# Neighbourhood attention: the modulation's product moved between value products and transposes, with a second row for its bias

## The reference, cut to what matters

```python
sh1, sc1, gt1, sh2, sc2, gt2 = ada_modulation(c, ada_w[i], ada_b[i])      # silu(c) @ ada_w + ada_b, 6 x 1024 wide
hl = modulate(rms_norm(xl, norm1_g[i]), sh1, sc1)
oc, ol = neighbourhood_attention(hc, hl, ...)   # layer 0: window of the 8 x 64 grid plus context, softmax, values
xl = xl + gt1 * ol
```

## Time and profile before

| | |
|---|---|
| median of 3 runs | 5085.33 us (5072.62 to 5091.82) |
| profiled execution | 5078.06 us, its span 5076.7 us |
| mean granted clock of TensorE | 0.958 of full speed |
| TensorE busy | 4573.2 us, 90% |
| VectorE, ScalarE, GpSimd busy | 1419.8, 1174.9, 270.6 us |
| the 48 units of attention | 1984.00 to 2215.08, 231.08 us |

### The profile page before, as it was taken

One profiled execution on the slowest core, in us unless ns is written; L12 is line 12 of the kernel. 1 busy time (PEld: TensorE's weight loads), 2 busy tenths in 40 slices (PEclk: granted clock), 3 DMA queues, 4 the chain that ended last, 5 costly groups with the idle time before them and its releaser, 6 DMA issues. The chain is left out here.

```text
span 5076.7 us, 86103 instructions
## 1 busy us (share of the span) xinstructions
PE 4573.2 (90%) x37006; PEld 2463.5 (49%) x37006; DVE 1419.8 (28%) x3516; ACT 1174.9 (23%) x2541; POOL 270.6 (5%) x418
## 2 busy tenths in 40 slices
PE   8999999989998899786999997996888888769998
PEld 6775444434444344543444443444666666534333
DVE  1032110020001221533222225133555555532223
ACT  2032111012101222423222221033333333321111
POOL 0000000000002002102000000022000000010000
PEclk9999999999999899997999998998999999979999
DMA  3143111121122113422777773233000000029998
GB/s 132 67 159 117 66 67 71 66 93 69 66 83 78 50 46 101 139 78 97 294 285 291 285 285 139 91 143 95 28 28 28 28 28 9 3 96 400 407 408 342
DMA packets 257924, 679.81 MB, mean 134 GB/s; under 512 B 23600, under 2 KB 66464, under 8 KB 257296
## 3 DMA queue, kind: packets, MB, share of 16 engines
q1 hardware_dynamic: 234048, 608.24, 32.4%
q0 software_dynamic: 23504, 66.07, 4.3%
HBM read 644.76 MB, written 26.74 MB: 132 GB/s over the span
## 5 line engine op out<-in xcount | busy, mean ns | idle before, releaser
L2197 PE MATMUL bank<-ring,arena 128*128 128x512 f32 x2592 | 1128.8, 596 | 17.1 <-DVE arena L1925 11.3
L2197 PEld LDWEIGHTS bank<-ring,arena 128*128 128x128 f32 x2592 | 559.7, 217 | 562.7 <-issue 477.6
L2566 PE MATMUL bank<-ring,arena 128*64 128x512 f32 x2048 | 470.2, 598 | 9.7 <-DMA ring<-in_moe_w 6.5
L2197 PE MATMUL bank<-arena,ring 128*128 128x512 f32 x1024 | 443.3, 595 | 1.5 <-ACT arena L1157 0.8
L1870 DVE TENSOR_TENSOR arena<-arena,bank 128x512 f32<-128x512 f32 x300 | 187.2, 683 | 649.2 <-PE bank L2539 580.3
L2197 PEld LDWEIGHTS bank<-arena,ring 128*128 128x128 f32 x1024 | 195.3, 191 | 247.1 <-issue 245.0
L2566 PEld LDWEIGHTS bank<-ring,arena 128*64 128x64 f32 x2048 | 139.5, 136 | 311.9 <-issue 308.6
L2592 PE MATMUL bank<-ring,arena 128*64 128x512 f32 x1024 | 232.0, 600 | 2.1 <-ACT arena L1375 1.6
L2368 PE MATMUL bank<-ring,arena 128*128 128x512 f32 x512 | 219.9, 592 | 0.0
L1368 ACT ACTIVATE arena<-bank 64x512 f32<-64x512 f32 x64 | 37.7, 590 | 662.3 <-PE bank L2566 662.3
L2829 PE MATMUL bank<-arena 64*64 64x128 f32 x3840 | 176.3, 302 | 1.0 <-issue 1.0
(11 more groups left out here) (403 smaller groups left out, 5412.2 us busy)
## 6 DMA issues: line engine op xcount, KB each, us to landing
ring<-in_moe_w SPq DMA_DIRECT2D x768, 512.0 KB, 7.5
ring<-in_w_in SPq DMA_DIRECT2D x21, 2048.0 KB, 7.7
ring<-in_ada_w SPq DMA_DIRECT2D x12, 2048.0 KB, 8.0
ring<-in_ada_w SPq DMA_DIRECT2D x24, 1024.0 KB, 5.4
ring<-in_w_up SPq DMA_DIRECT2D x8, 2048.0 KB, 8.1
ring<-in_w_down SPq DMA_DIRECT2D x8, 2048.0 KB, 7.6
ring<-in_na_w_qkv SPq DMA_DIRECT2D x6, 2048.0 KB, 7.9
ring<-in_w_in SPq DMA_DIRECT2D x8, 1024.0 KB, 6.4
```

Of the source, the lines that this page charges most:

```text
L2197: ins = mm(ps[:, 0:ncol], lhs(k), rhs(k), start=(k == 0 and first), stop=(k == nk - 1))
L2566: ins = mm(ps, x_chosen[:, b, k, 0:CAP_L], w[x][:, n * W:(n + 1) * W], start=(k == 0), stop=(k == KD - 1))
```

## The change

On TensorE the modulation's product of an odd iteration moves from the iteration's end, behind the shares, to a place between the value products and the transposes; the plan of banks is reordered in the same way, so that in bank 7 the product follows the shares of unit i-2, and the shares of unit i-1 follow the product. VectorE's and ScalarE's streams keep their order. The modulation's rows of layer 1 become two: the second lies in the last 256 columns of the ring slot whose upper half holds the shares. Its bias is loaded ahead of the loop, and `store_mod(1, n)` now loads the bias of product n+2. Since the second half of the second output weight overwrites that place, SP also waits, ahead of it, until all 36 stores of both modulations have landed.

```diff
@@ def plan_jobs():
         if i >= 2:
             plan.add("dve", "na_out", i - 2, bank=6)
+        if ada_beside_na(i) is not None:
+            plan.add("dve", "ada", 1, ada_beside_na(i), bank=7)
         if 1 <= i <= NA_UNITS:
             plan.add("act", "na_pt", i - 1, width=2, bank=4)
             plan.add("act", "na_share", i - 1, bank=7)
-        if ada_beside_na(i) is not None:
-            plan.add("dve", "ada", 1, ada_beside_na(i), bank=7)
@@ buffers
+    na_rows = ring[0:2, (first_na + 1) % RING, SLOT - ADA_COLS[1]:SLOT]
-    ada_rows = [[junk[0:2, b * W:(b + 1) * W] for b in range(2)], [n.take(ADA_COLS[1])[0:2, :]]]
+    ada_rows = [[junk[0:2, b * W:(b + 1) * W] for b in range(2)], [n.take(ADA_COLS[1])[0:2, :], na_rows]]
@@ SyncE, loads of weights
                 if first_na_o <= i < first_na_o + 2 and at:
                     taken(sp, *(("na_score", NA_UNITS - NT - 1) if i == first_na_o else ("na_out", NA_UNITS - 1)))
+                    if i > first_na_o:
+                        sp.wait_ge(sem("mod_stored"), 16 * (ADA_JOBS[0] + ADA_JOBS[1]))
@@ GpSimd
         load_bias(1, 0)
+        load_bias(1, 1)
         for n in range(ADA_JOBS[1]):
             store_mod(1, n)
@@ TensorE, loop over units
                 close(ins, "na_out", j)
+            if ada_beside_na(i) is not None:
+                ada(1, ada_beside_na(i))
             j = i - 1
             if 0 <= j < NA_UNITS:
                 ps = open_("na_pt", j)
@@
                 close(ins, "na_share", j)
-            if ada_beside_na(i) is not None:
-                ada(1, ada_beside_na(i))
```

## The result

The changed kernel takes 5041.98 us (median of 4 runs, 5035.5 to 5046.89), the kernel before, in the same set of runs, 5086.31 (4 runs, 5072.62 to 5091.82): a ratio of 0.9923, 95% interval 0.9906 to 0.994, so 39 us saved by the ratio and 44 by the medians. Forecast were 5048.0 us and 37.3 saved, in a range of 5026 to 5068.

What follows compares the result with a forecast made beforehand. TensorE, busy 90% of the span, was taken as the bound, so its stops in the attention stage count. Savings of 25.6+11.3+0.4=37.3 us from the median 5085.33 give 5048.0 us, range 5026 to 5068.

Steps and rivals of the forecast that it cites:

- The move: Attention stage: moving the product removes TensorE's wait for the shares' copy, adds one for VectorE's additions; saves 25.6 us.
- the replay: Step-by-step recalculation of a head pair's six iterations from measured start-to-start steps; 3.16 us saved for a pair.
- k=1: Unit 1 of a head pair's six, odd iteration: 4.60 us instead of 5.94, saving 1.34.
- k=4: Unit 4 of a head pair's six: keeps its 3.05 us, nothing saved.
- k=0: Unit 0 of a head pair's six: maxima start earlier, 3.47 us instead of 4.31, saving 0.84.
- The second row: Attention stage: a second bias row ends VectorE's waits for late bias loads; saves 11.3 us, bounds 0 and 11.3.
- The tail: Stage's end: the load of the modulation's rows goes out about 0.4 us earlier; saves 0.4 us.
- SP's new wait: Ahead of the second half of the last output weights: costs 0, or a few us without the first half's cover.
- A: Rival, odd iterations: additions release the shares later, taking the copy's place; 5073.6 us, no change; chance 0.19.
- k=3: Unit 3 of a head pair's six, with window: 4.94 us instead of 5.94; transposes hide all but 0.24 of the new wait.
- B: Rival, bias rows: congestion is the trouble, so the 11.3 us come back at the next user; 5059.3 us; chance 0.07.
- C: Rival, bias strips: they land late, VectorE stands in all 14 maskings and the clock falls; about 5109 us; chance 0.04.

Runs made afterwards that it cites:

- run 1: The changed kernel with the second bias row and SP's wait only, product still behind the shares: 5070.08 us, ratio to before 0.9995; repeated 5069.59 us, 0.9985.
- run 3: The changed kernel with VectorE's four additions done twice, first into unused columns of bank 7: 5075.35 us, ratio to the kernel before 0.9994.
- run 2: The changed kernel with the product's move only, keeping one bias row: 5058.37 us, ratio to the kernel before 0.996.
- run 4: The changed kernel measured again, unaltered, in two further sets: 5047.87 us (ratio to the kernel before 0.9941) and 5051.67 us (0.9949).
- run 6: The changed kernel with the product ahead of the values and VectorE's additions ahead of its attention product: 5042.26 us, ratio to the kernel before 0.9925.

## Why the prediction was right

**The bound.** TensorE's own stops in the stage decide. Shown: the stage lost 38.3 us and these are the stops and the lower clock that went, while VectorE's busy time in the stage hardly changes (118.89 and 117.97) and ScalarE's grows (116.74 and 120.18).

**The move, 25.6 forecast.** Between the row alone and the changed kernel lie 27.8 us (220.64 to 192.86). The seven later pairs, product to product, give 23.4 of them (191.30 to 167.91) against 22.1 forecast, the first pair and the ends 4.4 against 3.5. (The four terms that the forecast names for the odd iteration before add up to 5.87, not to the 5.94 measured; the 0.07 left over lie ahead of the values, and the replay has them, since it starts from the measured 1.29.) The replay was 0.15 too long for a pair, by small errors of both signs: the hand-over from the additions to the shares is 0.05 and not the 0.14 taken from the reciprocal's (k=1, 3 and 5 came out 0.18, 0.08 and 0.11 shorter; in k=1 VectorE is also free 0.08 earlier), while k=4 has the 0.20 for ScalarE and k=0 the 0.08 later maxima.

**The second row, 11.3 forecast.** 10.5 by the trace (run 1). Its price was taken from the distance of products over the whole stage and not from the waits' own length; that came out near the measured size. What the forecast did not say is how the parts hang together: it priced the row at the pace of the kernel before. At the new pace it is worth 18.9 (211.79 to 192.86), and the move without it 19.4. The sum holds only in the order in which it was made, row first. The stores in the traces are slow, 4.3 us in the median before and 4.1 in run 2, and run 2 shows 11 waits for the one row. The Trainium skill ("DMA: Bandwidth & Descriptors", Anatomy of one DMA) gives about 2.0 us of fixed cost. By an estimate from that figure one row would have done; the traces do not agree with it.

**The tail, 0.4 forecast.** It did not come: 5.62 from the last attention product's end to the turn, 5.49 before. The load went out only 0.13 earlier and not 0.4 (0.55 against 0.68 after the last attention product), and its landing varies by more than that. So this term was mis-sized, by little. SP's new wait cost nothing, as forecast: the second half of the last output weight goes out 0.03 us after the last attention product in both kernels.

**The rivals.** A falls by k=3, where the wait costs 0.16, and run 3 shows about what it would have cost. B falls by runs 1 and 2: a second row takes the late rows away and nothing comes in their place. C falls by the list of waits: VectorE waits for no strip in any of the changed kernel's three profiles.

**The total.** 37.3 forecast, 38.3 in the stage. The stage is where the forecast was right, three times over. That the timed saving was also near it, 39 us, is in part luck: the same kernel saved 30 and 26 us in the two repetitions, less than forecast, by what differs behind the stage (run 4).

**What stays open.** Whether the clock's fall in the recurrence has to do with the change, or came by chance in 4 of 7 profiles and in none of 5. The same question stands for all of the time behind the stage: in the five profiles of kernels with one part of the change or none it is 2858.0 to 2863.2 us, in those of the changed kernel, run 3 and run 6 it is 2859.5 once and 2869.3 to 2876.8 four times. No run separates an effect of the change there from chance. And the timed worth of the row alone, 0.9995 and 0.9985, of which the intervals agree with a little over nothing as well as with 10 us.

## What to carry to other kernels

Where a small product shares a bank with two other users, put it where its former holder has long been read, and then count its own reader as the gate of the next holder: here a microsecond more on VectorE gave back 25.2 of the stage's 38.3 us. A chain of store, landing, load and landing on one buffer sets a least distance between its rounds; measure it before the loop around it is shortened, since a buffer that is nearly in time now is late in almost every other round then (11 of 24). And replay the iteration from start-to-start rows, engine by engine: six lengths came out within 0.2 us each.

## What was not expected of the hardware

The same stop of 0.90 us, at the same instruction, is followed by a granted clock of 1.00 in some executions and of 0.50 for some 17 us in others. The six times of run 6 fall into two groups over 10 us apart (5033.5 to 5036.9 and 5047.7 to 5052.2). The fall does not explain them: the profiled execution is of the longer group (5047.66) and has no fall there. So a gain of 5 to 10 us is read in the stage that it touches and hardly from a few timed runs. The 2 KB loads of the bias land later in the changed kernel: medians of 2.6 to 2.9 us in the three profiles of the changed kernel, at 167 GB/s in the first, against 1.6 to 1.9 in those of the kernel before and of run 1; The traffic alone does not sort them: run 6, at 170 GB/s, has 2.8 for one row and 1.8 for the other, and run 2, at 152, has 2.3. Whether it is where the loads fall beside the weights' was not tried.
